# Second attention in waves inside the input projections, and rope from swapped projection columns

## What is computed

```python
qa, ka, va, oa, gates, qb, kb, vb = jnp.split(h @ w_in[l], IN_SPLITS, axis=-1)
...
h_a = (from_heads(h_a) * g_head_a[l] * jax.nn.sigmoid(oa.astype(f32))).astype(x.dtype)
h_b = from_heads(neighborhood_attention(to_heads(qb, NH_B), to_heads(kb, NH_B),
                                        to_heads(vb, NH_B), rpb[l])).astype(x.dtype)
mixed = jnp.concatenate([h_a, h_b], axis=-1) @ w_out[l]
```

```python
q = (rms_norm_2(cq, q_norm_g) @ w_uq).reshape(B, S, MLA_HEADS, QK_NOPE_DIM + QK_ROPE_DIM)
kv = (rms_norm_2(ckv, kv_norm_g) @ w_ukv).reshape(B, S, MLA_HEADS, QK_NOPE_DIM + V_HEAD_DIM)
...
def apply_rope(x, cos, sin):
    x1, x2 = jnp.split(xf, 2, axis=-1)
    return jnp.concatenate([x1 * cos - x2 * sin, x1 * sin + x2 * cos], axis=-1)
```

## Time and profile before

| | |
|---|---|
| median of 3 runs | 2654.15 us (2652.26 to 2656.86) |
| profiled execution | 2657.52 us, span 2655.7 us |
| busy: PE | 2456.4 us, 92% |
| busy: PE weight loads | 2121.0 us, 80% |
| busy: DVE | 1996.0 us, 75% |
| busy: ACT | 1119.2 us, 42% |
| mean granted clock of PE | 0.976 of 2.4 GHz |
| DMA | 620.11 MB, 234 GB/s on average |
| chain that ended last | PE 87%, DVE 8%, issue 2%, DMA 2%, ACT 1% |

### The profile page before, as it was taken

How to read it: one execution, slowest core, us unless ns; L and a number is a source line. 1 busy time by engine, 2 the same in 40 slices (tenths; PEclk the granted TensorE clock), 3 DMA queues, 4 the chain that set the end, 5 groups by cost and what they waited for, 6 DMA issues and landing times.

```text
span 2655.7 us, 33706 instructions
## 1 busy us (share of the span) xinstructions
PE 2456.4 (92%) x13756; PEld 2121.0 (80%) x13756; DVE 1996.0 (75%) x2495; ACT 1119.2 (42%) x1382; POOL 11.4 (0%) x12
## 2 busy tenths in 40 slices
PE   1599999788999999999997999999999988999996
PEld 1488888677888888888886888888888876888875
DVE  7988899678888777777787777777777667745545
ACT  1143534334545434444444444534553334534432
POOL 0000000000000000000000000000000000000000
PEclk9999999899999999999998999999999999999988
DMA  8878667555777688666674888666777754642232
GB/s 332 325 281 318 234 243 266 186 197 199 257 260 260 227 284 280 233 236 233 235 265 173 310 303 289 235 231 248 256 255 259 264 203 169 221 142 96 96 129 110
DMA packets 117723, 620.11 MB, mean 234 GB/s; under 512 B 13248, under 2 KB 14400, under 8 KB 73280
## 3 DMA queue, kind: packets, MB, share of 16 engines
q1 hardware_dynamic: 69408, 446.22, 47.7%
q10 hardware_dynamic: 48160, 171.73, 17.6%
HBM read 615.80 MB, written 2.10 MB: 233 GB/s over the span
## 4 chain that ended last, share of the span: by engine, by line
PE 87%; DVE 8%; issue 2%; DMA 2%; ACT 1%; POOL 0%; POOLq 0%; SPq 0%; ACTq 0%; DVEq 0%; PEldq 0%
PE pm L510 29%; PE ps L510 15%; PE pm L511 15%; PE ps L511 7%; PE pm L532 2%; PE pm L534 2%; PE pm L533 2%; DVE acc_first L1228 2%; PE pv L487 1%; PE ps L532 1%; PE ps L534 1%; PE ps L533 1%; DVE nt L1257 1%; DMA mixw<-in_mix 1%; DVE h L1263 1%
## 5 line engine op out<-in xcount | busy, mean ns | idle before, releaser
L1174 DVE TENSOR_TENSOR w_lo<-raw,w_hi 128x2048 fp32r<-128x2048 f32 (+1 forms) x408 | 891.8, 2186 | 326.1 <-ACT w_hi L820 324.7
L510 PE MATMUL pm<-h,w_hi 128*128 128x512 f32 x2640 | 938.7, 399 | 22.2 <-DVE h L1263 18.4
L820 ACT ACTIVATE w_hi<-raw 128x2048 fp32r<-128x2048 f32 (+1 forms) x408 | 745.4, 1827 | 398.9 <-DMA raw<-in_w_down 131.2
L511 PE MATMUL pm<-h,w_lo 128*128 128x256 f32 x2640 | 739.2, 280 | 0.0
L510 PEld LDWEIGHTS pm<-h,w_hi 128*128 128x128 f32 x2640 | 498.9, 189 | 144.1 <-issue 17.7
L511 PEld LDWEIGHTS pm<-h,w_lo 128*128 128x128 f32 x2640 | 500.6, 190 | 0.2
L510 PE MATMUL ps<-h,w_hi 128*128 128x512 f32 x1328 | 469.4, 397 | 0.0
L1189 DVE SCALAR_TENSOR_TENSOR acc<-ada,csil,acc 128x512 f32<-128x512 f32 x600 | 449.9, 750 | 13.6
L511 PE MATMUL ps<-h,w_lo 128*128 128x256 f32 x1328 | 370.3, 279 | 0.0
L510 PEld LDWEIGHTS ps<-h,w_hi 128*128 128x128 f32 x1328 | 249.2, 188 | 62.4 <-issue 3.6
L511 PEld LDWEIGHTS ps<-h,w_lo 128*128 128x128 f32 x1328 | 250.1, 188 | 0.0
(11 more groups left out here) (347 smaller groups left out, 2978.0 us busy)
## 6 DMA issues: line engine op xcount, KB each, us to landing
ada<-in_ada ACTq DMA_DIRECT2D x320, 512.0 KB, 5.4
raw<-in_w_up SPq DMA_DIRECT2D x88, 1024.0 KB, 4.9
raw<-in_w_in SPq DMA_DIRECT2D x56, 1024.0 KB, 5.8
raw<-in_w_down SPq DMA_DIRECT2D x64, 704.0 KB, 5.3
raw<-in_sgu_v SPq DMA_DIRECT2D x32, 1024.0 KB, 5.6
raw<-in_sgu_u SPq DMA_DIRECT2D x32, 1024.0 KB, 5.0
raw<-in_sgu_z SPq DMA_DIRECT2D x32, 1024.0 KB, 4.9
raw<-in_sgu_out SPq DMA_DIRECT2D x32, 1024.0 KB, 4.9
```

What stands on the lines that cost most here:

```text
L510: pe.matmul(dst[:, :], wh[:, k, :], hl, start=(kc == 0), stop=False, skip_group_check=True)
L511: mm = pe.matmul(dst[:, 0:T], wl[:, k, :], hi, start=False, stop=last, skip_group_check=True)
L820: act.activation(w_hi[:, q % HSLOTS, 0:n], raw[:, q % SLOTS, 0:n], ACT.Copy).then_inc(hi_ready, 1)
L1174: tt_(w_lo[:, q % SLOTS, 0:n], raw[:, q % SLOTS, 0:n], whole(w_hi[:, q % HSLOTS, 0:n]), ALU.subtract).then_inc(lo_ready, 1)
```

## The change

It has two parts that share nothing but the file.

In the input projections the order becomes `ka`, `qa`, `va`, `qb`, `kb`, `vb`, `oa`. The steps of both attentions now hang on single pieces: `A_STEPS` from `va` 7 to `vb` 2, about five pieces for a head, and `B_WAVES`, ten waves from `vb` 3 to `oa` 5. In wave w, after the named piece, PE transposes head w-1, multiplies head w-2 with the values and computes the scores of head w. DVE scales head w-1 inside `begin`, directly after the split (`urgent`), and ACT exponentiates it after its own. The second attention has buffers of its own (`s_b`, `pt_b`) and leaves its results in `ob` (the place of `qb`); the first leaves its own in `an` (the place of `qa`) and is gated after `oa` is there. Of the second attention's eight chunks, six are split into `hx`, during `oa` 6 and 7, the other two and the eight gated ones into `h` behind the projections. The first column block of `w_out` takes chunks 8 to 15 before 0 to 7. The conditioning pieces are spread by a new table, `bias_b` and the mask are loaded at the start by ACT, and the bias addition stands at `qa` 4.

In the latent heads the weights of a head get 64 more columns, the rotary ones with their halves swapped. The projection gives both in one product of 128 columns, one DVE multiplication by `turn` (cosines over signed sines) makes `qr`, and the rotary key is doubled over 128 rows by a matmul with `twice`. Rotation matmul and stage 1 are gone; a head has four stages. The query latent's last chunk is used on all 128 rows, with zero weights in the upper 64.

```diff
-HEADW = NOPE + ROPE + NOPE + VD
+HEADW = NOPE + 2 * ROPE + NOPE + VD
-W_IN = ["ka", "qa", "va", "oa", "qb", "kb", "vb"]
+W_IN = ["ka", "qa", "va", "qb", "kb", "vb", "oa"]
-ADA_SPANS = [("ka", 0, "w_out", 12, 8, 20), ("w_up0", 0, "w_up0", 40, 20, 24), ("w_down0", 0, "w_down0", 32, 24, 27),
...
+ADA_SPANS = [("ka", 0, 16, 26), ("va", 0, 8, 14), ("qb", 0, 16, 20), ("vb", 0, 15, 16), ("w_out", 0, 13, 20),
...
-W_IN_STEPS = {at: (("scores", "mix", "norm")[n % 3], n // 3) for n, at in enumerate(
-    [("va", 1)] + [(part, c) for part in ("oa", "qb", "kb") for c in (1, 3, 5, 7)][:11])}
+A_STEPS = {("va", 7): ("scores", 0), ("qb", 1): ("mix", 0), ("qb", 3): ("norm", 0),
...
+B_WAVES = {("vb", 3): 0, ("vb", 4): 1, ("vb", 5): 2, ("vb", 7): 3, ("oa", 0): 4, ("oa", 1): 5, ("oa", 2): 6, ("oa", 3): 7,
+           ("oa", 4): 8, ("oa", 5): 9}
...
# PE
+            def b_wave(w):
+                if 0 <= w - 1 < NH_B:
+                    hd_ = w - 1
+                    pe.wait_ge(b_probs, hd_ + 1)
+                    for sc in range(TT):
+                        for tt in range(TT):
+                            mm = pe.transpose(px[hd_ % 4][:, sc * T + tt * P:sc * T + (tt + 1) * P],
+                                              s_b[hd_ % 2][:, tt, sc * P:(sc + 1) * P], ident[:, :])
+                    mm.then_inc(b_pt, 1)
+                if 0 <= w - 2:
+                    hd_ = w - 2
+                    pe.wait_ge(b_ptsb, hd_ + 1)
...
+                        mm = pe.matmul(px[hd_ % 4][:, 0:T], vb[:, sc, hd_ * DH_B:(hd_ + 1) * DH_B], pt_b[hd_ % 2][:, sc, :],
+                                       start=(sc == 0), stop=(sc == 1))
+                    mm.then_inc(b_num, 1)
+                if w < NH_B:
...
+                        mm = pe.matmul(px[w % 4][:, tt * T:(tt + 1) * T], qb[:, w, tt * P:(tt + 1) * P], kb[:, w, :],
+                                       start=True, stop=True)
+                    mm.then_inc(b_scores, 1)
+            for c in range(KC):
+                columns("w_out", c, mixed, (lambda g: pe.wait_ge(mix_ready, 2 * (g + 1))) if c == 0 else None,
+                        order=[*range(8, KC), *range(8)] if c == 0 else None)
...
# PE, latent heads
-                            rows = slice(0, P) if kc < 3 else slice(64, P)
-                        pe.matmul(B[:, 0:T], rot, qr[j], start=True, stop=True).then_inc(m_rot, 1)
-                    elif st == 2:
                         pe.wait_ge(m_rope, hn + 1)
+            def doubled_key():
+                pe.wait_ge(kr_ready, 1)
+                pe.matmul(px[1][:, T:2 * T], twice, kr1, start=True, stop=True).then_inc(kr_twice, 1)
# ACT
+            act.wait_ge(unit_summed, FIRST_UNITS)
+            act.dma_start(flat(bias_b[:, :, :]), a["bias_b"]).then_inc(bias_in, 16)
...
-                        act.activation(qn[j], A[:, 0:T], ACT.Copy)
-                        act.activation(qr[j], A[0:ROPE, T:2 * T], ACT.Copy)
+                        act.activation(qn[j], A[:, 0:T], ACT.Copy).then_inc(m_qn, 1)
                         act.activation(kv[j], B[:, :], ACT.Copy).then_inc(m_proj, 1)
# DVE
+            def begin(stage, j=0, urgent=None):
                 q = piece(stage, j)
                 if q + AHEAD < TOTAL:
                     split(q + AHEAD)
+                if urgent is not None:
+                    urgent()
...
+            mix_low(h[:, 14:16, :], ob, 6, 4)
+            gated(3)
+            for p in range(4):
+                mix_low(h[:, 2 * p:2 * p + 2, :], oa, 2 * p, 5 + p)
...
-                        dve.wait_ge(m_rot, hn + 1)
-                        tt_(rt[j], B[0:ROPE, 0:T], sin, ALU.mult)
-                        chain.link(tt_(qr[j], qr[j], cos, ALU.mult))
-                        tt_(qr[j], qr[j], rt[j], ALU.add).then_inc(m_rope, 1)
+                        dve.wait_ge(m_qn, hn + 1)
+                        tt_(qr[j], A[:, T:2 * T], turn, ALU.mult).then_inc(m_rope, 1)
```

More of the change, by code:

```diff
@@ L330, in build @@
         b_num = sem("b_num")
[L331 removed]
+        b_out = sem("b_out")
+        mix_hi = sem("mix_hi")
         half_out = sem("half_out")
@@ L488, in sums, with columns @@
                     mm.then_inc(unit_summed, 1)
-            def columns(stage, c, src, need=None, late=None):
+            def columns(stage, c, src, need=None, late=None, order=None):
                 n = UBASE[stage] + c
@@ L504, in columns @@
                     wh, wl = (halves(w[:, s, 0:count * P], count) for w, s in ((w_hi, q % HSLOTS), (w_lo, q % SLOTS)))
-                    for k in range(count):
+                    for n_, k in enumerate(order or range(count)):
                         if need is not None and kc % 4 == 0:
                             need(kc // 4)
-                        hl, hi = src(kc)
-                        last = part == parts - 1 and k == count - 1
+                        hl, hi = src(kc - n_ + k)
+                        last = part == parts - 1 and n_ == count - 1
                         pe.matmul(dst[:, :], wh[:, k, :], hl, start=(kc == 0), stop=False, skip_group_check=True)
@@ L537, in tokens @@
                     mm.then_inc(piece_done, 1)
+                    if after is not None:
+                        after(4 * blk + part)
             def sum_first(u):
@@ L672, in _ @@
-            pe.wait_ge(mix_ready, 4 + NH_B)
-            stage_columns("w_out")
+                if (part, j) in B_WAVES:
+                    b_wave(B_WAVES[part, j])
+            for part in W_IN:
+                if part in TOKENS:
+                    for blk in range(TOKENS[part]):
+                        tokens(part, blk, after=lambda j: w_in_after(part, j))
+                else:
+                    for c in range(8):
+                        columns(part, c, both(h))
+                        w_in_after(part, c)
@@ new lines, in b_exponent, with mix_high @@
+            def b_exponent(w):
+                act.wait_ge(b_negmax, w + 1)
+                j = w % 2
+                for tt in range(TT):
+                    ex = act.activation(s_b[j][:, tt, :], s_b[j][:, tt, :], ACT.Exp, bias=small_b[:, j, 1, tt:tt + 1],
+                                        accum_out=small_b[:, j, 2, tt:tt + 1])
+                ex.then_inc(b_exp, 1)
+            def mix_high(dst, src, c):
+                act.activation(dst, src[:, c:c + 2, :], ACT.Copy).then_inc(mix_hi, 1)
@@ L1359, in _, with gated, mix_low @@
+            def gated(p):
+                dve.wait_ge(oa_gated, 2 * p + 2)
+                pair = oa[:, 2 * p:2 * p + 2, :]
+                tt_(pair, pair, an[:, 2 * p:2 * p + 2, :], ALU.mult).then_inc(a_gated, 1)
+            def mix_low(dst, src, c, n):
+                dve.wait_ge(mix_hi, n)
+                tt_(dst[:, :, T:2 * T], src[:, c:c + 2, :], whole(dst[:, :, 0:T]), ALU.subtract).then_inc(mix_ready, 1)
             w_in_dst = {"ka": ka, "qa": qa, "oa": oa, "qb": qb, "kb": kb}
             gate_step(0)
[L1361 to L1376 removed]
@@ L1377, in _ @@
+            for part, j in W_IN_PIECES:
+                w = B_WAVES.get((part, j), 0)
+                begin(part, j, (lambda: b_scale(w - 1)) if 0 < w <= NH_B else None)
+                if part == "ka" and j in (0, 1):
+                    gate_step(j + 1)
+                if (part, j) == ("qa", 0):
+                    gate_step(3)
+                if (part, j) == ("qa", 4):
                     dve.wait_ge(bias_in, 16)
@@ new lines, in _ @@
+                if (part, j) == ("oa", 7):
+                    mix_low(hx[:, 4:6, :], ob, 4, 3)
+                if part not in TOKENS:
+                    second_half(part, j, w_in_dst[part][:, j, :])
+                if (part, j) == ("oa", 6):
+                    mix_low(hx[:, 0:2, :], ob, 0, 1)
+                    mix_low(hx[:, 2:4, :], ob, 2, 2)
+                    for p in range(3):
+                        gated(p)
+                if (part, j) in A_STEPS:
+                    step, k = A_STEPS[part, j]
+                    {"scores": a_head_scores, "mix": a_head_mix, "norm": a_head_norm}[step](k)
@@ L1412, in _ @@
+                if (part, j) in B_WAVES and B_WAVES[part, j] < NH_B:
+                    b_arguments(B_WAVES[part, j])
+            mix_low(h[:, 14:16, :], ob, 6, 4)
+            gated(3)
+            for p in range(4):
+                mix_low(h[:, 2 * p:2 * p + 2, :], oa, 2 * p, 5 + p)
             clear_squares()
```

371 lines of the change are left out of this document (170 added, 201 removed), and 3 rows, old and new, of the table A_STEPS.

## The result

| | before | after |
|---|---|---|
| median of the runs | 2653.2 us (4 runs, 2651.8 to 2656.9) | 2591.5 us (4 runs, 2590.2 to 2595.6) |
| profiled execution, span | 2657.52, 2655.7 us | 2591.12, 2588.3 us |
| busy: PE, DVE, ACT | 92%, 75%, 42% | 93%, 77%, 43% |
| chain that ended last: PE, DVE | 87%, 8% | 87%, 9% |

The ratio is 0.9765, with a 95% interval of 0.9753 to 0.9778: 62 us faster, where 56 were forecast.

The account below looks back on a forecast made before the run. PE, busy 92%, was taken as the bound. Second attention and front -30.8, latent heads -17.2, drain -8.8, doubled key +0.5 make -56.3 us from 2657.52: 2601.2 profiled, less 3.4 for the median, 2598 us; range 2585 to 2620.

Parts of the forecast that it names:

- The gap: PE's gap between the last projection matmul and the first of `w_out`, second attention alone: 54.8 us removed.
- My chain of 5.3 us: Second attention's waves: scores to probabilities take about 5.3 us against a piece of 5.66, fitting with 0.3 to spare.
- The waves' work: Second attention's matmuls and transposes put back on PE between projection pieces: 8 x 2.2 = 17.8 us, at full clock.
- The tail: Behind the last projection piece, DVE's serial work delays the end of the first `w_out` piece: +2.2 us, bounds 0.5 and 4.
- The conditioning pieces: Moved forward, 26 in 16 slots of `ka` and `qa`, they load DVE more: +2 us, range 0 to 8.4.
- The latent heads: Up to the last head projection's end: rotation and 64-row surplus go, a small wait comes: net -17.2 us.
- slower: Latent heads: the shorter pipeline exposes projection, copy, multiplication, with low clock, at every step; total 2661 us, chance 0.03.
- The sign that was to prove this part wrong: Latent heads: a wait near a microsecond before scores L810, or steps above 10 us.
- The drain: From the last head projection to `mla_out`: 9.7 us instead of 18.5, so -8.8 us.
- 64 rows cost nothing: Latent heads: the surplus of scores and projection comes from something that stays; total 2612 us, chance 0.12.
- front bound by transfers or DVE: `ka` to `va` become bound by transfers or DVE, transfers adding +12.5 us; total 2610 us, chance 0.12.
- the waves wait: Second attention: the softmax chain doesn't fit in a piece, eight waves wait 2.5 us each; total 2618 us, chance 0.09.

Follow-up runs that it names:

- not_urgent: Changed kernel with DVE's scaling of the probabilities behind the conditioning pieces instead of directly behind the split; ratio to the kernel before 0.9793.
- waves_only: Kernel before with only the input-projection part (new order, attention in waves, new conditioning table), latent heads as before; ratio to the kernel before 0.9858.
- keys_first: Changed kernel with ACT copying a latent head's keys and values as two operations, keys first, signal behind the keys; ratio to the kernel before 0.9773.
- rows64_grouped: Changed kernel with rotary score products and last latent chunk on 64 rows, both plain score products first, then both rotary; ratio to the kernel before 0.9807.
- queries_early: Changed kernel with one signal more, so that ACT copies a head's queries before its projection piece ends; ratio to the kernel before 0.9753.
- wave0_later: Changed kernel with waves 0, 1, 2 of the second attention behind `vb` 4, 5, 6 instead of 3, 4, 5; ratio to the kernel before 0.9754.
- heads_only: Kernel before with only the latent-head part (swapped rope columns, four stages, doubled key, 128 rows); ratio to the kernel before 0.9897.
- rows64: Changed kernel with the rotary score products and the last query latent chunk on 64 rows again; ratio to the kernel before 0.9824.
- even_table: Changed kernel with its 96 first conditioning pieces spread evenly over 68 weight pieces from `ka` 0 to `w_out` 12; ratio to the kernel before 0.9809.
- w_out_natural: Changed kernel with the first column block of `w_out` in the order 0 to 15 instead of 8 to 15 first; ratio to the kernel before 0.9792.

## Why the prediction was right, step by step

The forecast was 2598 us, and 2591.5 came. In the profiled executions the difference is 67.4 us where the sum had 56.3. Of the 11.1 us between, 4.8 lie in the middle, which the change hardly touches, 3.3 at the waves and 2.5 at the latent heads.

**The gap** (-54.8) went whole, and the cover held: no wait before L643 in the changed kernel. That was close: in seven of the eight heads the scaling ends only 0.2 to 1.1 us ahead of PE, and 1.5 us more turn into six waits (`not_urgent`). My chain of 5.3 us was too long. I had added ACT's exponentials and DVE's split, but they run side by side (for head 1 ACT's from 439.20 to 440.31, DVE's from 439.08 to 441.36), and from the start of the arguments to the end of the scaling 4.6 us pass (437.49 to 442.09).

**The waves' work** was forecast at 17.8, with 1 for waits and 1 for the first attention, 19.8 in all; 16.5 came. The work was sized too high: a full wave sets the next dense matmul back by 1.98 us, and all ten together, without waits and without the sums of conditioning units that stand beside two of them, by 15.7. That is 1.96 for a head against 2.2. Then two errors of about the same size hid each other. I took one microsecond for the softmax chain, which isn't exposed. Instead wave 0 waits 2.05 for the norm of the first attention's last head, a wait that my sum hadn't, and the low clock behind it costs 1.7: 3.8. But the profile of before had a stall of the same size in that stretch (2.09 us before L487 at 394.20, with 3.4 us of low clock behind it), which I had left in and which is gone. Full clock was right for the waves, as the window 443:514.5 shows.

**The tail** (+2.2) measured +2.5 over the whole of `w_out`, but that is partly luck. The first piece, which the walk along DVE was about, takes 7.07 us (514.49 to 521.56) instead of 5.66, so +1.4. The other 1.1 are spread over the later pieces, a piece without a sum taking 5.62 us instead of 5.55 at the same granted clock; of that difference in pace more below.

**The conditioning pieces** were forecast at +2 and show +1.3 between `ka` and `va`. Of these 1.3 the low stretch at 156, which before hadn't, is about all: six executions of other kernels have the same code and no low clock there (`waves_only`, `keys_first`, `not_urgent`, `rows64_grouped`, `queries_early`, `wave0_later`), and take 140.2 to 140.9 us, where before took 140.5. So the pieces themselves cost nothing there, against the 2 of my sum. And the view was too narrow: I priced only where the pieces go to. The even table costs 8.7 us against the new one, some 7 without the clock's part, so this edit carries a part of the gain that my sum gave to the waves alone.

**The latent heads** (-17.2): rotation 0.52 as taken; scores' surplus 0.70 for 0.61, last chunk 0.22 for 0.29, wait 0.16 for 0.1. That makes 16.5, and with the clock's part taken out of the two executions 16.3 were measured. The rest of the -19.7 is the low clock at the first heads. I had read it and counted it only against the change, as the rival "slower"; it was a loss of before that could also go, and a term of 3.4 us belonged in the sum's range on the other side.

The sign that was to prove this part wrong, a wait near a microsecond before the scores L810, showed at the first head (1.02) and weaker at the second (0.67), where the pipeline is still filling and no value product stands in front. From the third on there is none, and the steps are 9.50. The sign should have been tied to the steps.

**The drain** was forecast at 9.7 us and took 9.5 (8.9 in `heads_only`, 9.9 in `wave0_later`).

The rival "64 rows cost nothing" is wrong, by `rows64`. By the rule of the Trainium skill that it leaned on (page "TensorE: Matmul & The Clock Gate", section "Back-to-back issue gap": time by columns) the scores would take the same time in all three kernels; they take 1.20, 2.06 and 1.67. My own reading, half of the products use 64 rows, named the place but not the cause: it is the change of rows. The rival "front bound by transfers or DVE" didn't come (`ka` to `va` took 141.8 us), nor did "the waves wait", which `not_urgent` and `even_table` show to be near. The slower rival needed 3.8 us per step; there were 0.16.

**The line that no step explains** (-4.3) is no gain. In all fourteen profiled executions, whatever the kernel, this stretch takes 1702.4 to 1707.6 us; before's 1706.6 lies within that, and the changed kernel's 1702.4 is the shortest of all. Over a part of it PE's matmuls follow each other more slowly in before, at the same granted clock 1.00. Before, then after, in `w_up1`:

```profile
1150.29 0.40 PE L510 MATMUL pm<-h,w_hi 128*128 128x512 f32 x1
...
1150.65 0.40 PE L510 MATMUL pm<-h,w_hi 128*128 128x512 f32 x1
```

```profile
1111.19 0.39 PE L515 MATMUL pm<-h,w_hi 128*128 128x512 f32 x1
...
1111.54 0.40 PE L515 MATMUL pm<-h,w_hi 128*128 128x512 f32 x1
```

A pair of matmuls takes 0.36 us against 0.35; most other executions of the changed kernel's variants have the slower pace there too. The medians differ by 61.7 us and the profiled runs by 66.4; this line is about as large as that difference.

## What to carry to other kernels

Where an engine stands still behind a stage, list what the stage's chain needs between two pieces of dense work, and put the urgent step directly behind the operation that everything waits for; a slack of 0.2 us was enough, and 1.5 us of other work in front of it was not. Background work should be kept out of the stretches where the helper engine is nearly full, even at the price of a small wait elsewhere. And products on fewer rows should stand together, or be padded with zeros to the full rows.

## What was not expected of the hardware

- Going from a product on 128 rows to one on 64 or back costs 0.22 to 0.24 us in f32 products (scores of 1.20, 1.67 and 2.06 us with no, two and four changes). The weight load then starts only with its product. Grouping halves the cost, and padding removes it. In the projection, where six products on 64 rows stand in a row, the two changes cost 0.22 together (7.33 us against 7.11).
- A stall costs more than its length: the wait at wave 0 was followed by 3.4 or 6.8 us at the low clock in eight of the ten profiled executions that have it, the 4.12 us of `w_out_natural` by 6.8.
- At a granted clock of 1.00 the pace of the same matmuls differs by 2% between executions, for some 200 us (0.353 us and 0.347 for a pair of 512 and 256 columns).
- A wait for two results that come together isn't shortened by one of them alone: in `keys_first` the keys come 0.21 us sooner (+0.86 instead of +1.07), and the step stays 9.50 us.
